# Input projection of a hybrid encoder block: two passes over tile pairs in Strassen's form

## What is computed

```python
h = rms_norm(x, norm_mix_pre)
z = h @ w_in                     # 1024 -> 512 q | 128 k | 128 v | 512 u | 512 v2
q, k = apply_rope(q), apply_rope(k)
a = window_sink_attention(q, k, v, attn_sinks)   # chunks of 64, window 128, 8 heads, 2 kv heads
g = gelu(z[..., 768:])
s = g_u * (W_s @ layer_norm(g_v) + b)            # blocks of 128 positions, 4 groups
x = x + rms_norm(concat(rms_norm(a), rms_norm(s)) @ w_out, norm_mix_post)
x = x + rms_norm(swiglu(rms_norm(x), w_gate, w_up, w_down), norm_ffn_post)
```

## Time and profile before

| | us |
|---|---|
| median of 3 runs | 1900.08 |
| profiled execution, its own time | 1901.72 |
| span of that execution, first to last instruction | 1899.9 |
| PE busy | 1860.3 |
| DVE busy | 1210.2 |
| ACT busy | 710.3 |
| POOL busy | 294.3 |

### The profile page before, as it was taken

One profiled execution on the slowest core, in us unless ns is written; L12 is line 12 of the kernel. 1 busy time (PEld: TensorE's weight loads), 2 busy tenths in 40 slices (PEclk: granted clock), 3 DMA queues, 4 the chain that ended last, 5 costly groups with the idle time before them and its releaser, 6 DMA issues. The chain is left out here.

```text
span 1899.9 us, 25241 instructions
## 1 busy us (share of the span) xinstructions
PE 1860.3 (98%) x9464; PEld 1542.3 (81%) x9464; DVE 1210.2 (64%) x1467; ACT 710.3 (37%) x1171; POOL 294.3 (15%) x230
## 2 busy tenths in 40 slices
PE   6999999989999899999999999999999999999998
PEld 5888888878888788888888788888888788888887
DVE  5444444464447787777777977677777756553564
ACT  6555555453335432322334332323233222222342
POOL 2222222221001111111111011111112000000243
PEclk9999999999999999999999999999999999999999
DMA  7111111144574533323335433223324754445665
GB/s 277 67 67 66 66 58 52 45 178 168 192 282 163 215 119 106 105 83 118 108 105 179 160 118 107 88 92 124 106 92 152 278 213 129 173 169 185 225 205 194
DMA packets 128823, 267.39 MB, mean 141 GB/s; under 512 B 5904, under 2 KB 84752, under 8 KB 119568
## 3 DMA queue, kind: packets, MB, share of 16 engines
q1 hardware_dynamic: 128784, 266.90, 40.5%
HBM read 186.66 MB, written 80.22 MB: 140 GB/s over the span
## 5 line engine op out<-in xcount | busy, mean ns | idle before, releaser
L1298 PE MATMUL T<-tb_hi,sb_hi 128*128 128x512 f32 x616 | 239.9, 389 | 1.6 <-DVE sb_lo L1184 1.6
L1299 PE MATMUL T<-tb_lo,sb_hi 128*128 128x512 f32 x616 | 239.7, 389 | 0.0
L1300 PE MATMUL T<-tb_hi,sb_lo 128*128 128x512 f32 x616 | 239.6, 389 | 0.0
L566 POOL TENSOR_TENSOR v<-u,p 128x512 f32<-128x512 f32 x44 | 116.0, 2637 | 725.4 <-DVE u L1068 725.4
L1047 DVE TENSOR_TENSOR t_lo<-t_raw,t_hi 128x1536 fp32r<-128x1536 f32 x132 | 221.8, 1734 | 0.1
L806 ACT ACTIVATE sb_hi<-sb_raw 128x1408 fp32r<-128x1408 f32 x56 | 77.4, 1382 | 291.2 <-PE T L1300 278.1
L1477 PE MATMUL ZB<-s_hi,t_hi 128*128 128x512 f32 x352 | 137.8, 391 | 3.6 <-DVE t_lo L1047 3.6
L1477 PE MATMUL T<-s_hi,t_hi 128*128 128x512 f32 x352 | 137.4, 390 | 1.3 <-DVE s_lo L1028 1.3
L1479 PE MATMUL ZB<-s_hi,t_lo 128*128 128x512 f32 x352 | 137.7, 391 | 0.0
L1478 PE MATMUL ZB<-s_lo,t_hi 128*128 128x512 f32 x352 | 137.6, 391 | 0.0
L1298 PEld LDWEIGHTS T<-tb_hi,sb_hi 128*128 128x128 f32 x616 | 115.7, 188 | 26.7 <-issue 2.2
(11 more groups left out here) (201 smaller groups left out, 4249.4 us busy)
## 6 DMA issues: line engine op xcount, KB each, us to landing
t_raw<-w_gu SPq DMA_DIRECT2D x44, 1024.0 KB, 4.7
act_d<-ac SPq DMA_DIRECT2D x22, 1792.0 KB, 8.0
sb_raw<-act_d SPq DMA_DIRECT2D x56, 704.0 KB, 4.1
h_d<-quarters SPq DMA_DIRECT2D x8, 1792.0 KB, 6.6
s_raw<-h_d SPq DMA_DIRECT2D x14, 1024.0 KB, 8.4
tb_raw<-w_dn SPq DMA_DIRECT2D x6, 1536.0 KB, 6.3
hT_raw<-x_t SPq DMA_DIRECT2D x16, 512.0 KB, 3.3
xt<-x SPq DMA_DIRECT2D x16, 512.0 KB, 3.9
```

The lines of the kernel that those rows point to most:

```text
L566: e.tensor_tensor(v22[:, :], u3[:, :], p5[:, :], ALU.add).then_inc(v22_done, 1)
L1298: e.matmul(out_ap, lhi, rhi, start=start, stop=False)
L1299: e.matmul(out_ap, lhi, rlo, start=False, stop=False)
L1300: return e.matmul(out_ap, llo, rhi, start=False, stop=stop)
```

## The change

- The input projection is made in two passes over the eight pairs of tiles. The first pass makes u and v2 for the pairs 7 down to 0 in the positions' order (j counts 0 to 7; the pair is 7 - j), with the spatial gate of each pair one pair later; it writes the second half of mix_d (mix_B). The second pass makes q/k/v and the attention for the pairs in rising order and writes the first half (mix_A).
- A pair is 2 tiles x 2 halves of K on the left, 2 halves of K x 2 halves of the columns on the right. Seven products stand for eight: 84 matmuls of 512 columns in the first pass, of 384 in the second. The opening pair (j = 0) of the first pass is made in plain products, 96 matmuls (uv_first).
- The norm's weights are now put on x instead of on w_in (scale_xq: on DVE for the opening pair, eight small ACT copies for each later pair). DVE forms the left sums (left_sums), ACT and DVE the seven high and low parts (left_hi, left_lo). The left parts of pairs j = 1 to 6 are stored in DRAM (store_hl to hl_d, 3.5 MB a pair) and loaded again for the second pass (load_hl_hi, load_hl_lo); those of j = 0 are formed again (again_*).
- DVE adds the products up (uv_u2, uv_u3, uv_corner, uv_upper, uv_lower; qkv_*, lower_right on POOL). Gelu reads the sums.
- The second pass's weights are loaded when pair j = 6 has ended; their sums, high and low parts are spread over the last pair of the first pass and the first of the second. The parts of w_out are made inside the last pairs of the second pass, and the last attention tiles are placed between the products of the first two output tiles (out_units).
- The loops of the first two stages are unrolled. Stage two is the same from output tile 2 on.

NP is 8, TILES 16. The core of the diff (uv_u2 and uv_u3 add products 2 and 3 to the saved product 0; uv_upper and uv_lower are one addition each from PSUM; stats_x is two Square operations with sums and one small copy; norm_stats is the layer norm's statistics and its subtraction; normed one operation):

```diff
-            def z_columns(out_ap, par, hi, lo, w):
-                for c in range(KD):
-                    ins = three(out_ap, hT_hi[par][:, chunk(c)], hT_lo[par][:, chunk(c)], hi[:, c, w],
-                                lo[:, c, w], c == 0, c == KD - 1)
-                return ins
...
+            for j in range(2, NP - 1):
+                load_xq(j + 1)
+                if j + 1 < NP - 1:
+                    store_hl(j + 1, 0)
+                store_mixB(j - 1)
+                if j + 2 < NP:
+                    load_xs(j + 2)
+                if j + 1 < NP - 1:
+                    store_hl(j + 1, 1)
+            e.wait_ge(in_done, 7 * (NP - 1))
+            e.wait_ge(hl_out, 64 * (NP - 2))
+            for q in (B11, B12, B22, B21):
+                e.dma_start(wq_in[q][:, :, :], w_qkv[q, :, :, :]).then_inc(w_in_loaded[q], 16)
...
+            e.wait_ge(w_sum, 4 + 3)
+            e.wait_ge(w_split, 9 + 1)
+            load_hl_hi(1)
+            store_mixB(NP - 2)
+            e.wait_ge(w_sum, 4 + 4)
+            e.wait_ge(w_split, 9 + 6)
+            load_hl_lo(1)
...
+            for j in range(NP - 1):
+                if j + 2 < NP - 1:
+                    e.wait_ge(in_done, 7 * (NP + j + 1))
+                    load_hl_hi(j + 2)
+                    load_hl_lo(j + 2)
...
+                if j == NP - 2:
+                    load_wout(3)
+                    load_wout(4)
+                    load_mix(0)
+                    load_mix(1)
+                    load_wout(5)
+                if j:
+                    store_mixA(2 * j - 1)
+                if j == NP - 2:
+                    load_wout(6)
+                store_mixA(2 * j)
+            load_wout(7)
...
+            def scale_xq(j):
+                q = lb_raw[j % 2]
+                e.wait_ge(xq_in[j % 2], 16 * (j // 2) + 16)
+                for kh in range(2):
+                    for k in range(HK):
+                        quads = q[:, 2 * kh:2 * kh + 2, k * P:(k + 1) * P]
+                        ins = e.activation(quads, quads, ACT.Copy, scale=gq[:, 8 * kh + k:8 * kh + k + 1])
...
+            def gelu_u(j, par):
+                r = rstdx[:, 2 * (NP - 1 - j) + par:2 * (NP - 1 - j) + par + 1]
...
+                elif par:
+                    e.wait_ge(v21_first, j)
+                    src = bv21[:, :]
...
+                e.activation(gu[par][:, :], src, ACT.Gelu, scale=r).then_inc(gel_done, 1)
...
+            for j in range(2, NP):
+                ahead = j + 1 < NP
                 if ahead:
+                    stats_x(j + 1)
+                uv_copy(j, 0)
+                if ahead:
+                    scale_xq(j + 1)
+                else:
+                    wq_hi_part(0)
+                uv_copy(j, 1)
+                if ahead:
+                    left_hi(j + 1, 0)
+                else:
+                    wq_hi_part(1)
+                    wq_hi_part(2)
+                squares_B(j - 1, 1)
+                gelu_v(j, 1)
+                if ahead:
+                    left_hi(j + 1, 1)
+                else:
+                    wq_hi_part(3)
+                gelu_u(j, 0)
+                squares_B(j - 1, 0)
+                mean_B(j - 1)
+                if ahead:
+                    left_hi(j + 1, 2)
...
+                gelu_v(j, 0)
+                if not ahead:
+                    wq_hi_part(5)
+                gelu_u(j, 1)
...
+            for j in range(NP):
+                p, last = j + 1, j + 1 == NP
+                if not last:
+                    qkv_copy(p, 0)
+                queries(2 * j)
+                if j:
+                    probs_half(2 * j - 1)
+                values(2 * j)
+                if j == NP - 2:
+                    wout_hi_part(2)
+                if j == NP - 3:
+                    again_hi(0)
+                if not last:
+                    qkv_copy(p, 1)
+                else:
+                    wout_hi_part(6)
+                    wout_hi_part(7)
+                exps(2 * j)
+                if j == NP - 2:
+                    wout_hi_part(3)
+                queries(2 * j + 1)
+                values(2 * j + 1)
+                if j:
+                    squares_A(2 * j - 1)
+                if j == NP - 3:
+                    again_hi(1)
+                probs_half(2 * j)
+                if not last:
+                    upper_left(p)
+                if j == NP - 2:
+                    mix_hi(0)
+                if last:
+                    mix_hi(1)
+                    mix_squares(0)
+                exps(2 * j + 1)
+                if j == NP - 3:
+                    again_hi(2)
+                if j in (2, 3):
+                    wout_hi_part(j - 2)
+                if j == NP - 2:
+                    wout_hi_part(4)
+                    wout_hi_part(5)
+                squares_A(2 * j)
+            x1_squares(0)
+            probs_half(TILES - 1)
+            squares_A(TILES - 1)
...
+            def left_sums(j):
+                q = lb_raw[j % 2]
+                e.wait_ge(xq_scaled, j + 1)
+                e.tensor_tensor(q[:, 4, :], q[:, 0, :], q[:, 3, :], ALU.add).then_inc(lsum_done, 1)
+                e.wait_ge(lsum_done, 4 * j - 3)
+                e.tensor_tensor(q[:, 5, :], q[:, 4, :], q[:, 1, :], ALU.subtract).then_inc(lsum_done, 1)
+                e.tensor_tensor(q[:, 6, :], q[:, 1, :], q[:, 0, :], ALU.subtract).then_inc(lsum_done, 1)
+                e.wait_ge(lsum_done, 4 * j - 2)
+                e.tensor_tensor(q[:, 7, :], q[:, 2, :], q[:, 5, :], ALU.subtract).then_inc(lsum_done, 1)
...
+            for j in range(2, NP):
+                ahead = j + 1 < NP
+                if ahead:
+                    left_sums(j + 1)
+                else:
+                    wq_sum(R1)
+                    wq_lo_part(0)
+                uv_u2(j)
+                if not ahead:
+                    wq_sum(R2)
+                gate(j - 1, 1)
+                uv_u3(j)
+                uv_corner(j)
+                if ahead:
+                    left_lo(j + 1, 0)
+                else:
+                    wq_sum(R3)
+                    wq_lo_part(1)
+                gate(j - 1, 0)
+                norm_stats(j, 1)
+                if ahead:
+                    left_lo(j + 1, 1)
+                uv_upper(j)
+                if ahead:
+                    mix_B(j - 1)
+                    left_lo(j + 1, 2)
+                normed(j, 1)
+                if not ahead:
+                    wq_sum(R4)
+                    wq_lo_part(2)
+                norm_stats(j, 0)
+                uv_lower(j)
+                normed(j, 0)
+            wq_lo_part(3)
+            mix_B(NP - 2)
...
+            def uv_product(j, i):
+                b, (left, _) = j % 2, UP_PRODUCTS[i]
+                if i < 2:
+                    e.wait_ge(lsplit, 3 * j + i + 1)
+                if i == 3:
+                    e.wait_ge(lsplit, 3 * j + 3)
...
+                for k in range(HK):
+                    w = slice(k * P, (k + 1) * P)
+                    hi, lo = lb_hi[b][:, left, w], lb_lo[b][:, left + 1, w]
+                    e.matmul(bank, hi, wu_hi[i][:, k, :], start=i < 4 and k == 0, stop=False, skip_group_check=True)
+                    e.matmul(bank, hi, wu_lo[i][:, k, :], start=False, stop=False, skip_group_check=True)
+                    ins = e.matmul(bank, lo, wu_hi[i][:, k, :], start=False, stop=k == HK - 1, skip_group_check=True)
+                ins.then_inc(in_done, 1)
...
+            def spatial(j, par):
+                n = 2 * j + 1 - par
+                if n == 0:
+                    e.wait_ge(pool_consts, 4)
+                e.wait_ge(vn_ready, n + 1)
+                if j == 0:
+                    e.wait_ge(gel_done, 4)
+                elif par:
+                    e.wait_ge(v21_first, j)
+                else:
+                    e.wait_ge(u2_first, j)
+                bank = GU[j % 2][2 + par]
...
+            for j in range(2, NP):
+                for i in range(7):
+                    uv_product(j, i)
+                    if i in (2, 4):
+                        spatial(j - 1, 1 - i // 4)
...
+            for j in range(NP - 1):
+                p = j + 1
+                qkv_product(p, 0)
+                turn_qk(2 * j)
+                if j:
+                    turn_probs(2 * j - 1)
+                qkv_product(p, 1, range(0, 2))
+                scores(2 * j)
+                qkv_product(p, 1, range(2, 4))
+                qkv_product(p, 2)
+                if j:
+                    weighted(2 * j - 1)
+                qkv_product(p, 3)
+                turn_qk(2 * j + 1)
+                qkv_product(p, 4, range(0, 2))
+                turn_probs(2 * j)
+                qkv_product(p, 4, range(2, 4))
+                scores(2 * j + 1)
+                if p == NP - 1:
+                    mix_transposes(0)
+                qkv_product(p, 5)
+                qkv_product(p, 6)
+                weighted(2 * j)
+            out_units(0, 0, 2)
```

(105 more changed lines are left out.)

1413 lines of the change are left out of this document (925 added, 488 removed).

## The result

The changed kernel takes 1947.71 us (median of 4 runs, 1943.56 to 1949.57) against 1900.77 of the kernel before beside it: a ratio of 1.0243 [1.0231, 1.0255]. I had predicted 1892, and 1906 at most. The profiled execution has a span of 1947.6 us, 47.7 more than before. The third output tile's first product starts at 491.49 where it stood at 443.23, 48.3 us later: all of the loss lies in the two passes and the ending behind them, nothing in the later stages.

A forecast was written before the change was run, and what follows sets the result against it. TensorE's stream was taken to bound the kernel. PE work -31 us, first pass waits +8, opening +3, change of pass +5, ending and second pass +7: 8 us less, 1892 us; eight in ten between 1873 and 1906.

The forecast's parts named there:

- Does the rest keep up? First pass: First pass: a ring over DVE and ACT sets a turn of 23.6 us, 2.1 more than PE needs; four turns 94.4.
- The ring that I did sum: First pass: DVE's 17.0 us up to uv_lower, then ACT's gelu, statistics, copy and scaling, 6.6 with hand-overs: 23.6 a turn.
- Rival (b): First pass, left_sums to scale_xq: full durations and slower mix_B make a turn 26.5 us, total time 1906 us; chance 0.14.
- TensorE's price of a pair: First pass: PE's own work on one pair, products and gates, takes 21.5 us.
- Products of 384 columns: Second pass: each such matmul costs 0.174 us on TensorE, read off the line through 512 and 256 columns.
- Six iterations: Second pass: six pairs at 23.3 us each, hand-overs just in time, 140 us.
- rival (a): Both passes: PE alone bounds the kernel, first pass at 21.5 us a pair, total time 1875 us; chance 0.17.
- The opening: Start of the first pass: scale_xq(3) ends at 74.5 us, about 20 us of PE lost against some 17 before.
- Change of pass: Between the passes: about 5 us lost, on low weight parts and the left quarters' reload; second pass starts at 222.
- The ending: From pair 6 of the second pass to the third output tile: 73 us, 13 of them lost; that tile starts at 435.
- Rival (c): Second pass: the reload of left quarters comes 2 us late, five times, total time 1902 us; chance 0.07.
- Rival (d): First pass, ACT: a table load before each Square that follows gelu, +6 us, total time 1898 us; chance 0.05.

The follow-up runs named there:

- experiment 1: Changed kernel with SyncE's x_q load issued right behind the first half of the split quarters' store: 1924.89 us, ratio 1.0123.
- experiment 9: experiment 8 with the store of the split quarters' second half put back ahead of the x_q load: 1907.95 us, ratio 1.0033.
- experiment 4: experiment 1 with the x rows also loaded early, and pair 3's loads ahead of pair 2's split stores: 1912.63 us, ratio 1.0062.
- experiment 8: experiment 4 plus ScalarE's scaling before last gelu and statistics, first bank copy before statistics, and output-weight chunks 3, 4, 7 ahead of mix stores: 1878.14 us.
- experiment 6: Changed kernel with only the output weight's chunks 3, 4 and 7 loaded ahead of the mix stores: 1937.0 us, ratio 1.0188.
- experiment 2: Changed kernel with only ScalarE's order altered, both bank copies ahead of the scaling: 1948.92 us, ratio 1.0251.

## Why the prediction was wrong

**The step that failed** is "Does the rest keep up? First pass". It followed one ring, over DVE and ACT, and let x_q be there whenever ScalarE came to it. SP's list was never walked: load_xq(j+2) stands behind store_hl(j+1,1), which waits for left_lo(j+1,2), and with the 3 MB just ahead of it the load takes 12 us to land. Nearly all terms of this second ring lay in rows that I had: 14.0 of DVE by the prices of the earlier trace rows, 4 MB at the 400 GB/s of the earlier trace rows, 10 us and 2 more, scaling 3.0: 29, and 30.4 with SP's 1.4 us of issuing, which only the new trace shows; 31.0 was measured. I used that bandwidth for the reload of the left quarters and for the second-pass weights, and not for the pass in which the new stores are made. Experiments 1 and 9 show it from both sides: the load moved out gives 23 us, one store put back in costs 30.

**The ring that I did sum** was right in its links and nearly in size: 24.4 for 23.6 with the loads early (experiment 4), DVE's part 17.1 for 17.0. It bound nothing in the changed kernel, as a longer one lay over it. Rival (b) had the right sign by the wrong mechanism: no longer operations, no slower mix_B; a full turn of DVE's work was as summed.

**TensorE's price of a pair** was 21.5 and is 20.9, read in experiment 8 between the issues of x_q, which wait for each pair's end. The turn of 20.2 there is no price of TensorE's: the four turns, read at the scaling, take 19.8, 19.8, 20.3 and 20.9 and close in on TensorE's pace, and they hold 384 matmuls where four pairs with their gates have 400. Products of 384 columns start every 0.173 us, for 0.174. Six iterations take 141.9 there, 144.0 in the changed kernel, for 140. These terms carry the gain, and they hold: 23 us of the gain come out in experiment 8, which at 1878 lands beside rival (a), 1875, PE alone; but (a) was said of the changed kernel's own order, and there it is false.

**The opening** came 11 us late by the same kind of cause, SP's list, but mostly by another load: ScalarE waits 7.7 us for pair 3's x rows, issued at 68.39 behind the stores of pair 2, and then 2.2 for x_q, issued at 73.00 behind mix_B(0) as well. With x_q alone early scale_xq(3) still ends at 84.1 (experiment 1); with both loads ahead of the stores of pair 2 at 76.1, for 74.5 forecast (experiment 4). So the rest of the opening was summed nearly rightly.

**Change of pass**: 56.4 for 53.1. TensorE waits in it 5.4 us for the last pair's bank copy, 4.0 for low weights and 2.2 for the gate, where I gave 5 in all. In experiment 8 it waits 4.9, but the stretch (55.9) starts there at a scaling that stands earlier in ScalarE's list, so the two are not the same work. Small, and not tested.

**The ending** had both mechanisms right (chunk 3 behind mix_A(10), chunk 7 behind mix_A(12)) and their sizes too small: I gave 2.5 and 4 us, together 6.5, and experiment 6 gave back 10.7. (My items of the ending add up to 12 us lost, where the sum has 13.) Part of the difference may be the clock: the granted clock is 0.92 over that stretch and 0.98 in experiment 8.

**Rival (c)**, the reload, is dead: TensorE waited 1.3 us in all for hl_d loads. **Rival (d)** too. ACT's group of table loads from 85 to 409 us, one before the second pass's first exp:

```profile
L911 ACT ACT_TABLE_LOAD x1 | 1.3, 1283 | 0.0
```

None stands beside the squares that follow gelu. The Trainium skill's "ScalarE: Activation LUTs" (Table sets: the hidden batching unit) leaves open which set squares belong to; here they ran in gelu's without a load.

**Left open:** how much of TensorE's low clock cost time by itself. It waited 5 to 7 us once a turn, and behind such a wait the window of the changed kernel reads

```profile
117.60:121.00 3.40, 3.34 (x8) 2.67 (x9) 3.37 (x8) 1.38 (x2) 0.00 (x0) 0.50 0.00 0
```

a granted clock of 0.50, the lower level of 1.2 GHz, with matmuls of 512 columns 0.43 us apart. In the first pass x_q's other condition, the end of a pair's products, was met by 93.5 (the next pair's first product starts at 93.45), some 7 us before SP came to it, so slow products there were probably covered by the ring. That is argued from the trace; no run tested it.

## What to carry to other kernels

When a change closes a buffer's ring over DRAM, walk the DMA list as one more engine: for each load, what stands ahead of it in the list, what those entries wait for, and how many bytes they put in front of it. Issue what the next turn needs ahead of stores that nobody waits for. And treat a releaser that the profile names as the last link only: in experiment 2 its wait changed its name and not its size; the engine whose long wait lies on the path that repeats (here DVE, 14 us a turn ahead of its left sums) is a better place to start reading backwards. The longest wait alone does not tell: POOL's, 20 us, held up nobody.

## What the runs showed of the hardware

The same 1 MB load took 12.5 (changed kernel), 9.1 (experiment 9), 8.5 (1) and 5.1 us (8) to land, while each kernel moved the same bytes in the pass: by what had been issued just ahead of it and was still under way. The granted clock fell to 0.50 behind single waits of 5 to 7 us in a stream that was otherwise dense, and read 1.00 in the same pass once those waits were gone (72.60 to 153.40 us of experiment 8). Shorter waits went either way: in experiment 1 it read 0.50 from 134 to 136 us, behind a wait of 2.03 us, and behind waits of 2.49 and 2.26 us the next twelve products ran at full pace.
